# Stick-breaking attention's strict mask by TensorE, its constant products in two exact parts; the modulation's sums by ScalarE and GpSimd in the projections

## What is computed

```
def stick_breaking(q, k, v, pos):          # 8 heads of 64
        z = jnp.einsum('bqhd,bkhd->bhqk', qb, k).astype(jnp.float32) * scale
        strict = pos[None, :] < qp[:, None]
        log_keep = jnp.where(strict, jax.nn.log_sigmoid(-z), 0.0)
        later = lax.cumsum(log_keep, axis=3, reverse=True) - log_keep
        a = jnp.where(strict, jnp.exp(jax.nn.log_sigmoid(z) + later), 0.0)
        return jnp.einsum('bhqk,bkhd->bqhd', a.astype(v.dtype), v)
...
    cond = jax.nn.silu(c)                   # 1024 values
        mod = cond @ w_ada[l] + b_ada[l]    # 1024 x 6144
        sh1, sc1, g1, sh2, sc2, g2 = jnp.split(mod, 6, axis=-1)
```

## Time and profile before

| | us |
|---|---|
| median of 3 runs (lowest, highest) | 2765.95 (2765.64, 2781.81) |
| the profiled execution's own time | 2779.04 |
| its span | 2777.2 |
| TensorE busy | 2492.1 (90% of the span) |
| VectorE, ScalarE, GpSimd busy | 1613.9, 859.1, 873.8 |
| projections (first chunk to the attention's first scores) | 21.24 to 204.82 |
| stick-breaking attention | 204.82 to 322 |

### The profile page before, as it was taken

One profiled execution on the slowest core, in us unless ns is written; L12 is line 12 of the kernel. 1 busy time (PEld: TensorE's weight loads), 2 busy tenths in 40 slices (PEclk: granted clock), 3 DMA queues, 4 the chain that ended last, 5 costly groups with the idle time before them and its releaser, 6 DMA issues.

```text
span 2777.2 us, 35683 instructions
## 1 busy us (share of the span) xinstructions
PE 2492.1 (90%) x14398; PEld 1975.2 (71%) x14398; DVE 1613.9 (58%) x3307; ACT 859.1 (31%) x1493; POOL 873.8 (31%) x787
## 2 busy tenths in 40 slices
PE   8999998898887787879899967799999999999999
PEld 7676565676444444468674556799999888888888
DVE  5247567552100000054536999899999876777775
ACT  3125333332000000033422248633333333333332
POOL 0003322001000100010001259655555565656662
...
GB/s 228 246 112 235 91 46 46 94 152 211 418 423 421 421 423 421 338 156 92 31 34 189 36 20 232 272 385 353 358 347 341 368 363 362 387 372 390 381 387 197
DMA packets 155097, 720.59 MB, mean 259 GB/s; under 512 B 15464, under 2 KB 30736, under 8 KB 125744
## 3 DMA queue, kind: packets, MB, share of 16 engines
...
q0 software_dynamic: 62832, 226.00, 21.2%
...
...
## 4 chain that ended last, share of the span: by engine, by line
PE 52%; DVE 26%; DMA 13%; ACT 4%; issue 3%; POOL 2%; SPq 0%; POOLq 0%; DVEq 0%; ACTq 0%
DMA arena<-w 8%; PE psum L3383 7%; PE psum L1656 5%; DVE rounded L3462 5%; DVE arena L3513 5%; PE psum L442 4%; PE psum L2721 4%; PE psum L2186 4%; DMA arena<-v_rows,arena 3%; PE psum L971 3%; PE psum L3372 3%; PE psum L1663 2%; DVE arena L3498 2%; PE psum L3320 2%; POOL arena L3309 2%
## 5 line engine op out<-in xcount | busy, mean ns | idle before, releaser
L3383 PEld LDWEIGHTS psum<-rounded,rounded 128*128 128x128 f32 x3072 | 456.5, 190 | 30.4 <-issue 14.2
L3383 PE MATMUL psum<-rounded,rounded 128*128 128x320 f32 x3072 | 468.3, 313 | 11.0 <-DVE arena L3506 7.0
L3372 PEld LDWEIGHTS psum<-rounded,rounded 128*128 128x128 f32 x2880 | 425.1, 189 | 15.6 <-issue 6.7
L3372 PE MATMUL psum<-rounded,rounded 128*128 128x320 f32 x2880 | 431.4, 311 | 0.4 <-DVE rounded L3462 0.4
L3309 POOL DMA_INDIRECT arena<-u_rows,arena x192 | 288.9, 1505 | 243.6 <-DVE arena L3513 139.6
L1656 PE MATMUL psum<-arena 128*64 128x256 f32 x2048 | 257.6, 415 | 79.9 <-issue 53.0
L3401 ACT ACTIVATE rounded<-arena 128x1024 fp32r<-128x1024 f32 x248 | 255.8, 1049 | 226.8 <-PE psum L3383 162.3
L3309 POOL DMA_INDIRECT arena<-v_rows,arena x192 | 257.3, 1340 | 167.1 <-DVE arena L3524 55.6
L3462 DVE TENSOR_TENSOR rounded<-arena,rounded 128x1024 fp32r<-128x1024 f32 x248 | 302.6, 1220 | 7.0 <-ACT rounded L3401 5.4
L1656 PEld LDWEIGHTS psum<-arena 128*64 128x64 f32 x2048 | 182.9, 150 | 166.2 <-issue 115.1
L1779 DVE COPY arena<-psum 128x256 f32<-128x256 f32 x32 | 13.6, 425 | 441.3 <-PE psum L1706 441.3
...
...
## 6 DMA issues: line engine op xcount, KB each, us to landing
...
xb<-arena SPq DMA_DIRECT2D x1, 12032.0 KB, 48.8
...
```

The source lines that it names most:

```text
L3372: ins = pe.matmul(PS[:, b, 0:DT], w[:, x, k, :], hv[:, y, :], k == 0 and i == 0, k == 7 and i == 2)
L3383: ins = pe.matmul(PS[:, b, 0:DT], w[:, y, x, :], gg[:, z, :], x == 0 and i == 0, x == 7 and i == 2)
```

## The change

The strict mask moves to TensorE: after each score product, a product of HUGE (2^100 on the diagonal) with TRIR puts -2^100 on the triangle, so that softplus and the exponential become zero there. GpSimd's 64 selects are gone. `PT` is split by VectorE into two parts (`parts_dv`: a rounding copy and a subtraction), and TRI, NEG and the selector are copied once to single-pass operands, so each product with them becomes two single-pass products. ScalarE's fourth softplus of a head moves behind its last exponential.

The modulation moves into the projections. SP fetches `w_ada` in 96 rows of 256 KB, into 3 places for the first row of a block and 5 for the others, between the `wp1` blocks; ScalarE scales each (5 behind each of the first 16 chunks' splits, 8 behind each of its two V evictions), GpSimd adds them (84 additions), TensorE does the one-column products at the ends of 12 chunks (`MOD_AT`) into bank 7, and VectorE adds the bias once. Banks are dealt anew for that. The zeros and `wp1[6]`, `wp1[7]` (gates) are fetched in the attention, and ScalarE waits for the zeros ahead of `gate_upper(0)`.

The diff, cut to its core (removed besides: VectorE's `sums`, the memset in `norm1_dv`, `ada_done`, `ada_at`, TensorE's one-column block in `stick_pe`):

```diff
+    TRIR, NEGR, SELR, HUGE = (alias(O_WORK - x, w)[:, :] for x, w in ((496, 128), (368, 128), (240, 240), (O_WORK - 2 * RING - 7936, 128)))
...
+        po.tensor_copy(TRIR, TRI).then_inc(*N1.po())
+        po.tensor_copy(NEGR, NEG).then_inc(*N1.po())
+        po.tensor_scalar(HUGE, IDENT, 2.0 ** 100, None, ALU.mult).then_inc(*N1.po())
+        po.tensor_copy(SELR, CST[:, C_SEL:C_SEL + 240]).then_inc(*N1.po("constants"))
...
+    MOD_AT = {2: 0, 4: 1, 6: 2, 7: 3, 8: 6, 10: 7, 12: 8, 13: 9, 15: 10, 16: 11}
+    MOD_STEPS = [5] * 16 + [0] * 5
...
     def proj_sp(sp):
-        for p, free in ((2, P.dv["split", 3]), (3, P.dv["split", 7]), (4, P.pe["vm"])):
-            if p == 4:
-                zeros_sp(sp)
-            sp.wait_ge(*free)
-            fetch(sp, p % 2, (p % 2) * RING, A["wp1"][p], "wp1", p)
+        def mod_pieces(a, b):
+            for n in range(a, b):
+                c, k = n // 8, n % 8
+                src = A["wada"][c][:, 512 * k:512 * k + 512]
+                if k == 0:
+                    if c >= SUM_PLACES:
+                        sp.wait_ge(*P.pe["mod", c - SUM_PLACES])
+                    sp.dma_start(out=MOD_SUM[c % SUM_PLACES], in_=src).then_inc(*d_mod_sum[c % SUM_PLACES]("piece", c))
+                else:
+                    x = 7 * c + k - 1
+                    if x >= ROW_PLACES:
+                        sp.wait_ge(*P.po["mod", (x - ROW_PLACES) // 7, (x - ROW_PLACES) % 7 + 1])
+                    sp.dma_start(out=MOD_ROW[x % ROW_PLACES], in_=src).then_inc(*d_mod_row[x % ROW_PLACES]("piece", x))
+
+        mod_pieces(0, 8)
+        sp.wait_ge(*P.dv["split", 3])
+        fetch(sp, 0, 0, A["wp1"][2], "wp1", 2)
+        mod_pieces(8, 28)
+        sp.wait_ge(*P.dv["split", 7])
+        fetch(sp, 1, RING, A["wp1"][3], "wp1", 3)
+        mod_pieces(28, 58)
+        sp.wait_ge(*P.pe["vm"])
+        fetch(sp, 0, 0, A["wp1"][4], "wp1", 4)
+        mod_pieces(58, 70)
         sp.wait_ge(*P.dv["split", 11])
         fetch(sp, 1, RING, A["wp1s"], "wp1s")
+        mod_pieces(70, 90)
         sp.wait_ge(*P.dv["split", 15])
         fetch(sp, 0, 0, A["wp1"][5], "wp1", 5)
-        sp.wait_ge(*P.dv["split", 16])
-        sp.wait_ge(*P.pe["wi"])
-        fetch(sp, 1, RING, A["wada"][0], "wada", 0)
-        sp.wait_ge(*P.dv["split", 20])
-        fetch(sp, 0, 0, A["wada"][1], "wada", 1)
-        sp.wait_ge(*P.pe["chunk", 20])
-        fetch(sp, 2, 2 * RING, A["wada"][2], "wada", 2)
+        mod_pieces(90, 96)
         sp.wait_ge(*P.dv["kin"])
         sp.wait_ge(*P.dv["rk"])
         sp.wait_ge(*P.dv["qi", 3])
...
+        def mod_columns(c):
+            pe.wait_ge(*P.po["mod", c, 7])
+            for k in range(4):
+                ins = pe.matmul(PS[:, 7, 4 * c + k:4 * c + k + 1], MOD_SUM[c % SUM_PLACES][:, 128 * k:128 * k + 128], ONE[:, 0:1], True, True)
+            ins.then_inc(*P.pe("mod", c))
...
+            if j in MOD_AT:
+                mod_columns(MOD_AT[j])
...
+        done = [0]
+
+        def mod_steps(count):
+            for n in range(done[0], done[0] + count):
+                c, k = n // 8, n % 8
+                x = 7 * c + k - 1
+                if k == 0:
+                    row, piece = MOD_SUM[c % SUM_PLACES], d_mod_sum[c % SUM_PLACES]["piece", c]
+                else:
+                    row, piece = MOD_ROW[x % ROW_PLACES], d_mod_row[x % ROW_PLACES]["piece", x]
+                ac.wait_ge(*piece)
+                ac.activation(row, row, ACT.Copy, scale=SC8[:, k:k + 1]).then_inc(*P.ac("scaled", c, k))
+            done[0] += count
+
         ahead(0)
         root_ac(ac)
...
             ahead(j)
+            mod_steps(MOD_STEPS[j])
...
+            mod_steps(8)
...
+            mod_steps(MOD_STEPS[j])
...
+        dv.wait_ge(*P.po["mod", 11, 7])
...
     def proj_po(po):
+        for c in range(12):
+            total = MOD_SUM[c % SUM_PLACES]
+            for k in range(1, 8):
+                po.wait_ge(*P.ac["scaled", c, k])
+                if k > 1:
+                    po.wait_ge(*P.po["mod", c, k - 1])
+                po.tensor_tensor(total, total, MOD_ROW[(7 * c + k - 1) % ROW_PLACES], ALU.add).then_inc(*P.po("mod", c, k))
         po.wait_ge(*P.pe["chunk", 19])
...
         ins.then_inc(*S.po("kmb"))
-        po.wait_ge(*S.po["kmb"])
-        for kt in range(4):
-            po.wait_ge(*S.dv["keep", 0, kt])
...
     def scores_of(pe, h):
         j, p0 = h // 2, 64 * (h % 2)
         for kt in range(4):
             c = META + 128 * kt
-            pe.matmul(region(h, kt, 128 * kt), KA[p0:p0 + 64, j, c:c + 128], QA[p0:p0 + 64, j, 128 * kt:T],
-                      kt < 3, False).then_inc(*S.pe("z", h, kt))
+            z = region(h, kt, 128 * kt)
+            pe.matmul(z, KA[p0:p0 + 64, j, c:c + 128], QA[p0:p0 + 64, j, 128 * kt:T], kt < 3, False)
+            pe.matmul(z[:, 0:128], HUGE, TRIR, False, False).then_inc(*S.pe("z", h, kt))
 
     def stick_sp(sp):
+        sp.wait_ge(*P.dv["split", 20])
+        fetch(sp, 0, 0, A["wp1"][6], "gates", 0)
         sp.wait_ge(*d_rot.end())
-        fetch(sp, 3, 3 * RING, A["wada"][3], "wada", 3)
-        for c in range(4, 12):
-            sp.wait_ge(*S.pe["ada", c - 4])
-            fetch(sp, PLACE[c % 4], PLACE[c % 4] * RING, A["wada"][c], "wada", c)
+        zeros_sp(sp)
+        sp.wait_ge(*S.pe["sel", 7])
+        fetch(sp, 1, RING, A["wp1"][7], "gates", 1)
         wait_all(sp, P)
-        for i in range(2):
...
+            halves_of = (PTH[i], PTL[i])
             for kt in (3, 2, 1, 0):
-                pe.wait_ge(*S.po["keep", h, kt])
-                ins = pe.matmul(region(h, kt, 128 * kt), TRI, PT[i][kt], False, kt == 3)
+                pe.wait_ge(*S.dv["lower", h, kt])
+                for x in range(2):
+                    ins = pe.matmul(region(h, kt, 128 * kt), TRIR, halves_of[x][kt], False, kt == 3 and x == 1)
                 for k2 in range(kt + 1, 4):
-                    ins = pe.matmul(region(h, kt, 128 * k2), NEG, PT[i][k2], False, k2 == 3)
...
                 ins.then_inc(*S.pe("later", h, kt))
                 for x in AFTER[kt]:
                     bank[3 * i + x % 3 if x < 3 else 3 * i + 1] = S.ac["a", h, x]
-            sel = CST[:, C_SEL + 112 - 16 * h:C_SEL + 240 - 16 * h]
+            sel = SELR[:, 112 - 16 * h:240 - 16 * h]
...
+                for x in range(2):
+                    ins = pe.matmul(PS[:, 7, 128 * kt:T], sel, halves_of[x][kt], False, h == 7 and kt == 3 and x == 1)
             ins.then_inc(*S.pe("sel", h))
-            c0, c1 = ada_done(h - 1) if h else 0, ada_done(h)
-            if h < 7:
-                claim(3 * i + 2)
-                for c in range(c0, c1):
-                    pe.wait_ge(*S.dv["ada", c])
-                    for k in range(4):
-                        ins = pe.matmul(PS[:, 3 * i + 2, 4 * (c - c0) + k:4 * (c - c0) + k + 1],
-                                        ada_at(c)[:, 0, 128 * k:128 * k + 128], ONE[:, 0:1], False, True)
-                    ins.then_inc(*S.pe("ada", c))
-                bank[3 * i + 2] = S.dv["mod", h]
...
+                if h < 7 and m < 3:
                     weights_ac(ac, h + 1, m)
...
+                weights_ac(ac, h + 1, 3)
             if h < 4:
...
+        ac.wait_ge(*d_zero.end())
...
+    def parts_dv(dv, h, kt):
+        dv.wait_ge(*S.dv["keep", h, kt])
+        dv.tensor_copy(PTH[h % 2][kt], PT[h % 2][kt]).then_inc(*S.dv("upper", h, kt))
+        dv.wait_ge(*S.dv["upper", h, kt])
+        dv.tensor_tensor(PTL[h % 2][kt], PT[h % 2][kt], PTH[h % 2][kt].bitcast(F32), ALU.subtract).then_inc(*S.dv("lower", h, kt))
+
     def stick_dv(dv):
         for h in range(8):
             if h < 7:
                 for kt in range(4):
                     weights_dv(dv, h + 1, kt)
-                    sums(dv, 3)
-                c0, c1 = ada_done(h - 1) if h else 0, ada_done(h)
-                dv.wait_ge(*S.pe["ada", c1 - 1])
-                dv.tensor_tensor(MOD[:, 4 * c0:4 * c1], PS[:, 3 * (h % 2) + 2, 0:4 * (c1 - c0)],
-                                 VEC[:, V_BADA + 4 * c0:V_BADA + 4 * c1], ALU.add).then_inc(*S.dv("mod", h))
...
     def stick_po(po):
-        for h in range(8):
-            for made, x in (("keep", 0), ("a", 2), ("a", 3), ("a", 1), ("keep", 1), ("a", 0), ("keep", 2), ("keep", 3)):
-                if made == "a":
-                    po.wait_ge(*S.ac["a", h, x])
-                    strict(po, EX[h % 2][x][:, 0:128], "a", h, x)
-                elif h < 7:
-                    po.wait_ge(*S.dv["keep", h + 1, x])
-                    strict(po, PT[(h + 1) % 2][x][:, 0:128], "keep", h + 1, x)
+        po.wait_ge(*P.pe["chunk", 20])
+        po.memset(ZERO, 0.0).then_inc(*S.po("zeros"))
         gate_lower(po, 0)
         wait_all(po, S)
```

123 lines of the change are left out of this document (58 added, 65 removed).

## The result

The changed kernel takes 2799.33 us (median of 11) against 2774.45 (median of 11) for the kernel before on the same chip: a ratio of 1.0087, 95% interval 1.006 to 1.0115. It is slower by 24.9 us, 0.9%; the prediction was 2760 us, 5.6 less than before, with 2783 as its upper end. Of the 39 us between 2760 and 2799.33, 8.5 lie in the starting value: the prediction started from 2765.95, the median of three executions.

The account below looks back on a forecast made before the run. TensorE was taken to bound the projections, TensorE and VectorE the attention. Attention gain 38.4 us, less 3 for the clock, against a projection loss of 29.8: -5.6 from 2765.95, so 2760 us, range 2733 to 2783.

Parts of the forecast that it names:

- One-column sums: Projections: the modulation's 12 one-column sums move onto a TensorE with nothing idle, 0.9 us each, a loss of 11.0 us.
- The walk of the sums: Projections: following GpSimd's chain of additions against TensorE's chunks, TensorE waits 13.7 us in all for late sums.
- the third rival: Projections: additions set the pace and the kernel gets slower, 2786 us at 1.70 us an addition; chance 0.13.
- Clock behind the waits: Projections: three of TensorE's waits for sums exceed 1.54 us and lower its clock, 1.7 us each, 5.1 in all.
- HUGE four: Attention, each head on TensorE: the four mask products with HUGE take 0.3 to 0.45 us together.
- TRI, NEG and selector: Attention, each head on TensorE: single-pass products take 2.6 to 2.9 us for TRI and NEG, 1.25 for the selector.
- The chain through ScalarE: Attention: softplus and exponentials outlast TensorE's 9.0 us a head, so a head takes 9.8 us and TensorE idles 0.8.
- the cover: Attention: VectorE's last part of a head comes 2.6 us before TensorE wants it, so its work is hidden.
- Clock in the attention: Attention: TensorE's gaps of 0.8 us a head lower its clock, charged 3 us in all, bounds 0 to 11.
- The clock falls in every head: Rival for the attention: the gain is 28 to 30 us instead of 35, giving 2767 us; chance 0.17.
- The adds set the pace: Projections: TensorE waits for sums 1, 3, 9 and 11, kernel slower, 2786 us at 1.70 us an addition; chance 0.13.
- The signs named: Profile signs: heads 9.8 us apart; head 1's scores near 234 us, beyond 245 if additions pace; splits near 1.9 us.

Follow-up runs that it names:

- e13: The changed kernel with each mask made by two single-pass products over the scores' 64 rows; 2785.23 us, ratio 1.0027 to the kernel before.
- e14: The changed kernel with GpSimd's 84 additions over 8 columns instead of 512, so mod is wrong; 2776.83 us, executed once.

## Why the prediction was wrong, step by step

The sum had -5.6 us and the two stretches gave +29.4, 35.0 more. By terms: in the projections 11.4 for the clock, 5.3 for the waits, 1.5 for the masks of head 0 and 0.2 for the one-column products; in the attention 8.8 for the clock and 6.5 for heads that are longer at full clock, mostly by their masks; and 1.3 for the later start. No term had the wrong sign. What failed are the prices of both clock terms, of the HUGE products, and of the landing of pieces behind a block.

- **One-column sums, +11.0.** Right: a sum takes 0.93 to 0.95 at full clock. At the low clock behind a wait it took 1.86 or 1.87, four times. (Where I wrote "12.1 plus the sums" for a head before, the 12.1 had their 0.88 in it already. The forecast goes by 117.2 and doesn't use it.)
- **Scores of head 0.** Left out. They stand among the projections, and their four masks make the stretch from them to the scores of head 1 19.83 us instead of 18.37: +1.5 of the loss that I never priced.
- **The walk of the sums, waits 13.7.** Mis-sized, 19.3 measured: 4.4 for sum 1, 5.5 for 3, 3.2 for 7 and 6.2 for 11, where I had 1.5, 5.3, 0.6 and 2.4. Sums 0 and 9, 3.9 us in my walk, didn't wait. The terms that failed are the landing of a piece behind a block and ScalarE's place in the line. I let the pieces come 6.5 us after the block's fetch; they came 9.1, 9.0, 9.6 and 10.9 us after it (34.73 to 43.82 for wp1[2], and so on). And I kept ScalarE a chunk ahead, while it stood 10.1, 8.0, 14.3 and 6.3 us, and VectorE's splits stood 62 us for ScalarE's. The longest, 120.5 to 134.8 us, starts before wp1[4] is even issued, at 125.24: pieces 58 to 69 stand behind the block, and the block behind SP's wait for `vm` (the waits of SP's queue, then its timeline):

```profile
SPq L280 <- PE psum L504: 9.0, 1, 9.0
```

```profile
125.24 0.33 SPq L280 DMA_DIRECT2D arena<-wp  x1
```

A scaling took 0.72 us, not 0.63, and a piece 3.2 us to land (median of the 96), where the third rival had taken 2.6. The additions themselves I had too dear: 109 + 33 = 142 us, against 123.6 measured, turns included.
- **Clock behind the waits, 5.1.** The step that failed most in the projections. With 11.2 for the one-column products, 1.5 for the masks and 19.0 of waits (19.3, and 1.1 for VectorE, less 1.4 before), 16.5 of the 48.2 us are left, and the missing clock rises by 20.5 us (part of it while TensorE stood). I took the 1.7 us behind a wait of 1.5 us in the earlier trace rows for each of three; around waits of 3.2, 4.4 and 5.5 us 3.4 were missing each time, twice that. Around the last it was 13.7, of which the narrow products had 3.4 in the kernel before: that the clock falls there with TensorE busy stands in the trace that I had, and I tied the clock to idle gaps alone.
- **HUGE four, 0.3 to 0.45.** Wrong by a factor of four: 1.53 us. I had taken a product's price from rows in which its neighbours have the same number of rows, and e13 shows that it holds there (0.11). I had no row in which 64-row and 128-row products alternate, where the weight load doesn't hide.
- **TRI, NEG and selector, 2.6 to 2.9 and 1.25.** Right, and near: 2.76 and 1.43. A 128-column product with its load takes the upper end, 0.11 (two in 0.22, 323.68 to 323.90).
- **The chain through ScalarE.** Right in kind: y waits for the last exponential, 0.36 instead of 0.8 us, since TensorE's part is longer. In e13, with the masks at the price that I had taken, the head is 10.1 us (9.8 predicted) and A 81.1 (78.8). VectorE's parts were never waited for; the cover was there.
- **Clock in the attention, +3 with 0 to 11.** It cost 11.8: at full clock A is 85.4 (six heads of 10.73, and 20.97 from the last scores to the end), measured 97.1. I had tied it to TensorE's idle gaps. It fell with no gap at all in four of the five heads, and e13, which has a gap of 0.36 or 0.45 us in every head, kept it at 1.00. That my upper bound of 11 came near is luck.
- **The rivals.** *The clock falls in every head* was nearest for the attention, though for another reason than its own. *The adds set the pace* was the right side of zero and named three of the four places (1, 3 and 11; 7 came instead of 9), but not for its reason: with the turns the walk has 142/84 = 1.69 us an addition, the rival more, and 1.47 was measured. What it named as a cause, a piece's landing, was the nearer part.
- **The signs named.** Scores of head 1 beyond 245 us (254.4) did mean late sums. Heads of 9.8 didn't come. Splits 1.72 and additions to 2.28 show the turns, as said.

What the earlier trace rows suggested, and the Trainium skill, "SBUF — State Buffer", section "Who interferes with whom", states, held in this case: additions against VectorE's two-input instructions lengthen both, and e14 gives VectorE's lengths without them, 761 and 1222 ns.

The Trainium skill, "TensorE: Matmul & The Clock Gate", section "What's actually happening", says that the clock follows how busy TensorE has been. The trace agrees behind the waits for sums 1, 3 and 7. It doesn't in the attention, if busy is read as the profile's busy share: that was 4.00 of 4.00 us at a granted clock of 0.50, and so it was at the narrow products of the kernel before.
